# A second product turned around, sparse rows for more tokens, and an earlier choice of experts (hybrid decoder layer, one core)

## What is computed

```python
def block(xb):                       # 128 tokens, 8 heads, top 16 of 128 x 128 experts
    qry = (xb @ w_q).reshape(TB, PEER_HEADS, PEER_D_KEY)
    s1 = jnp.einsum('thd,nd->thn', qry[..., :half], keys_1)
    s2 = jnp.einsum('thd,nd->thn', qry[..., half:], keys_2)
    v1, i1 = lax.top_k(s1, K)
    v2, i2 = lax.top_k(s2, K)
    cand = (v1[..., :, None] + v2[..., None, :]).reshape(TB, PEER_HEADS, K * K)
    sc, ci = lax.top_k(cand, K)
    idx = (take(i1, ci // K) * PEER_N_KEYS + take(i2, ci % K))
    gate = jax.nn.softmax(sc, axis=-1)
    act = jax.nn.gelu(jnp.einsum('thed,td->the', u_table[idx], xb), approximate=False)
    return jnp.einsum('the,thed->td', gate * act, v_table[idx])
```

## Time and profile before

| | |
|---|---|
| three runs | 1499.63, 1503.68, 1505.55 us, median 1503.68 |
| the profiled execution | 1502.88 us, its span 1501.1 us |
| mean granted clock of TensorE | 0.991 of full speed |
| busy share: PE, DVE, POOL, ACT | 98%, 78%, 45%, 43% |
| DMA | 410.28 MB, 273 GB/s on the mean |
| TensorE instructions of the second product | 2304 matmuls of 512 columns |
| TensorE instructions of the first product | 3072 of 352 columns, 768 of 128 |

### The profile page before, as it was taken

How to read it: one execution, slowest core, us unless ns; L and a number is a source line. 1 busy time by engine, 2 the same in 40 slices (tenths; PEclk the granted TensorE clock), 3 DMA queues, 4 the chain that set the end, 5 groups by cost and what they waited for, 6 DMA issues and landing times.

```text
span 1501.1 us, 23329 instructions
## 1 busy us (share of the span) xinstructions
PE 1467.1 (98%) x8045; PEld 1304.6 (87%) x8045; DVE 1174.9 (78%) x2373; ACT 640.7 (43%) x1055; POOL 672.8 (45%) x390
## 2 busy tenths in 40 slices
PE   7999989899999999999999999999999999999998
PEld 6879658788999999999999999988888888888887
DVE  4747473278999999989899899568878878877876
ACT  4463453222333333457777766433233233224221
POOL 2423140133586678865455454134433433443441
PEclk9999979999999999999999999999999999999999
DMA  7400202220569989999999999699999999999993
GB/s 263 148 29 1 113 1 74 85 85 16 191 224 351 328 307 351 412 376 358 370 366 375 373 358 387 238 378 376 386 350 354 346 347 352 347 352 349 350 344 123
DMA packets 183961, 410.28 MB, mean 273 GB/s; under 512 B 12852, under 2 KB 108852, under 8 KB 182360
## 3 DMA queue, kind: packets, MB, share of 16 engines
q1 hardware_dynamic: 142296, 258.46, 48.6%
q0 software_dynamic: 41600, 151.03, 26.5%
HBM read 361.12 MB, written 48.30 MB: 273 GB/s over the span
## 4 chain that ended last, share of the span: by engine, by line
PE 79%; DVE 9%; DMA 7%; POOL 2%; issue 1%; ACT 1%; SPq 0%; DVEq 0%; ACTq 0%; POOLq 0%
PE banks L1987 21%; PE banks L1760 16%; PE banks L2055 12%; PE banks L2056 12%; PE banks L2057 12%; DMA u_rows<-in_u,idx 7%; DVE gate_rows L1621 3%; DVE u_rows L1566 2%; POOL u_lo L739 2%; PE banks L2026 1%; PE banks L1968 1%; DVE u_lo L1549 1%; DVE oh L1617 1%; PE banks L1787 1%; PE banks L1832 1%
## 5 line engine op out<-in xcount | busy, mean ns | idle before, releaser
L787 POOL DMA_INDIRECT v_rows<-in_v,idx x128 | 204.2, 1596 | 325.5 <-DVE x_res L1705 273.9
L2055 PE MATMUL banks<-v_hi,w_hi 128*128 128x512 f32 x768 | 298.9, 389 | 0.0
L2056 PE MATMUL banks<-v_lo,w_hi 128*128 128x512 f32 x768 | 298.8, 389 | 0.0
L2057 PE MATMUL banks<-v_hi,w_lo 128*128 128x512 f32 x768 | 298.8, 389 | 0.0
L1118 ACT ACTIVATE v_hi<-v_raw 128x1024 fp32r<-128x1024 f32 x128 | 126.4, 1050 | 327.0 <-PE banks L2057 294.5
L755 POOL DMA_INDIRECT u_rows<-in_u,idx x160 | 189.2, 1182 | 137.6 <-DVE z L1566 105.2
L1643 DVE TENSOR_TENSOR v_lo<-v_raw,v_hi 128x1024 fp32r<-128x1024 f32 x128 | 153.4, 1219 | 96.3 <-ACT v_hi L1118 96.3
L739 POOL TENSOR_TENSOR u_lo<-u_raw,u_hi 128x1024 fp32r<-128x1024 f32 x66 | 164.6, 2497 | 86.4 <-ACT u_hi L1004 46.0
L1987 PE MATMUL banks<-h_lo,u_hi 128*128 128x352 f32 x1024 | 196.2, 326 | 0.0
L1987 PE MATMUL banks<-h_hi,u_hi 128*128 128x352 f32 x1024 | 189.2, 327 | 0.0
L1987 PE MATMUL banks<-h_hi,u_lo 128*128 128x352 f32 x1024 | 184.2, 322 | 2.8 <-DVE u_lo L1549 2.8
(11 more groups left out here) (277 smaller groups left out, 2086.9 us busy)
## 6 DMA issues: line engine op xcount, KB each, us to landing
u_raw<-in_uT SPq DMA_DIRECT2D x128, 512.0 KB
v_raw<-in_v SPq DMA_DIRECT2D x128, 512.0 KB
gate_scratch<-stage SPq DMA_DIRECT2D x12, 2048.0 KB
gates<-gate_scratch SPq DMA_DIRECT2D x29, 768.0 KB
act_scratch<-act_out SPq DMA_DIRECT2D x116, 176.0 KB
act_in<-act_scratch SPq DMA_DIRECT2D x29, 704.0 KB
wi_raw<-in_w_in SPq DMA_DIRECT2D x8, 1024.0 KB, 7.0
wq_raw<-in_w_q SPq DMA_DIRECT2D x8, 1024.0 KB, 5.7
```

The costliest lines, as they stand in the source:

```text
L787: nc.gpsimd.indirect_dma_start(v_rows[s % V_ROWS][:], None, v_flat, bass.IndirectOffsetOnAxis(ap=idx0[:, s:s + 1], axis=0)).then_inc(vg_in ...
L2055: mm(y, w, v_hi[q][:, j, ds], start=first and j == 0, stop=False)
L2056: mm(y, w, v_lo[q][j][:, ds], start=False, stop=False)
L2057: end = mm(y, w_lo[q][:, j, t * P:(t + 1) * P], v_hi[q][:, j, ds], start=False, stop=last and j == GROUP - 1)
```

## The change

**Second product turned.** v becomes stationary, w moves: per group 8 chunks of the width x 4 blocks x 3 passes = 96 matmuls of 352 columns. The result is y transposed, 8 chunks in 8 banks (`Y_BANKS` has eight; the chunk's columns NE to ND hold the 352 tokens). At the end ACT copies each chunk to `yT`, TensorE turns it by 24 transposes (`turn`) into six banks, and DVE adds these to x; x is stored in six half tiles, not three whole ones.

**Sparse v rows for the 32 tokens.** Their gates no longer go to DRAM: CHUNKS 12 -> 11, BATCHES 96 -> 88 (the last trip of the gate stage has 8 batches, the last four blocks before POST none), the weights have 352 columns. Instead 32 more gathers bring v rows (kind "w"); DVE scales and sums them in `acc_b` (z1 x g1 as the scale; g1 comes by 4 small DMAs on SP's queue before the gate stage), and 8 matmuls with `fold` add the four groups of 32 partitions into the y banks before the last group. Kind "v" is block 0's v rows. One list `ALL_DOTS` now orders all 320 gathers; 10 of "w" stand in POST (1, 1, 1, 1, 2, 2, 1, 1), the other 22 and 128 of "v" in groups 1 to 30, five in each.

**Block 0 chosen early.** Score jobs become `s0` (block 0, emptied by DVE) and two `s13` (block 1; blocks 2 and 3), which ACT copies to SBUF. DVE does block 0's top-k of a head with those of block 1 and of one earlier head of block 2; after head 3 it chooses experts of the first four heads of block 0, and POOL starts gathering. The rest of the top-k's and choosing is spread over the first product's blocks (`routing`). Eight dots lie in the query stage, 72 in blocks 0 to 71 and 80 in the gate stage (before: 0, 71, 81, and 8 in POST). POOL makes u_lo of blocks 0 to 31 alone and gathers between. wq_lo gets three buffers; the last wq_lo stands on POOL's queue behind `idx_ready` and four gathers.

The diff, cut to its core:

```diff
-CHUNKS = ND // CHUNK
+CHUNKS = NA // CHUNK
-BATCHES = ND // BATCH
+BATCHES = NA // BATCH
-POOL_FIRST, SHARE_FROM = 16, 20
+POOL_FIRST, SHARE_FROM = 32, 32
+EARLY = 8
+for _n in [x for x in range(30) if x % 3 < 2]:
+    DOTS[_n] = "a"
-for _n in [*range(PRE - 25, PRE, 2), *range(PRE + 1, PRE + 32, 2), PRE + 4, PRE + 14, PRE + 24]:
+for _n in [*range(PRE - 19, PRE, 2), *range(PRE + 1, PRE + 32, 2), *range(PRE + 4, PRE + 28, 4)]:
     DOTS[_n] += "b"
-for _n in [*range(PRE - 14, PRE, 4), *range(PRE + 32, POST)]:
+for _n in range(PRE + 32, PRE + 44):
     DOTS[_n] += "a"
+POST_ADDS = [1, 1, 1, 1, 2, 2, 1, 1]
+ALL_DOTS += "w" * (NE - ALL_DOTS.count("w")) + "v" * SLOTS
+FREE_PIECE = 2650
 PIECE_SIZE = 1800
-Y_BANKS = (4, 5, 6, 7, 0, 1)
+Y_BANKS = (4, 5, 6, 7, 2, 3, 0, 1)
...
-        jobs += [(("s12", h, i), "D") for i in range(2)]
+        jobs += [(("s0", h), "D")] + [(("s13", h, i), "A") for i in range(2)]
...
@@ gpsimd
+            for h in range(PH - 1):
+                split_query(h)
+            pool.wait_ge(idx_ready, 1)
+            for s in range(U_ROWS // 2):
+                gather_u(s)
+            split_query(PH - 1)
+            for s in range(U_ROWS // 2, U_ROWS):
+                gather_u(s)
             for n in range(POOL_FIRST):
                 split_u(n)
+                if n < EARLY:
+                    gather_u(U_ROWS + n)
+                elif DOTS[n - EARLY]:
+                    gather_u(U_ROWS + dots_before(n - EARLY))
...
@@ scalar, after the heads' scores
+                free(copy(scores_1[:, h, :], bank(j)[:, 0:2 * NK]), j)
+                free(copy(scores_23[:, :, h, :], bank(j).rearrange("p (t e) -> p t e", t=2)), j)
...
+                if h + 2 == PH:
+                    for b in (2, 3):
+                        emptied(act, LAST_ON[b])
+                    nc.scalar.activation(h2_first, h2_nat[:, 0, :], ACT.Copy).then_inc(h2_placed, 1)
...
+            for c in range(KD):
+                act.wait_ge(y_done, c + 1)
+                copy(yT[:, c, :], ps[:, Y_BANKS[c], 0:ND]).then_inc(yT_ready, 1)
...
@@ vector
+            for h in range(PH // 2):
+                top_k(0, h)
+                top_k(1, h)
+                if h:
+                    top_k(2, h - 1)
+            for _ in choose(0, 0, PH // 2):
+                pass
+            top_k(2, PH // 2 - 1)
+            for h in range(PH // 2, PH):
+                top_k(0, h)
+                if h > PH // 2:
+                    top_k(1, h - 1)
+                if h >= PH - 2:
+                    for _ in range(EARLY // 2):
+                        dot()
...
-                nc.vector.tensor_copy(w32[:, :, 0:NE], head).then_inc(w_ready, 1)
...
@@ tensor, second product
-                for o in range(6):
+                for c in range(KD):
+                    if last and c == 6:
+                        turn(0, range(4))
+                    if last and c == 7:
+                        turn(1, (4, 5))
+                    ds = slice(c * P, (c + 1) * P)
+                    y = ps[:, Y_BANKS[c], NE:ND]
                     for j in range(GROUP):
-                        w = w_hi[q][:, j, t * P:(t + 1) * P]
-                        mm(y, w, v_hi[q][:, j, ds], start=first and j == 0, stop=False)
-                        mm(y, w, v_lo[q][j][:, ds], start=False, stop=False)
+                        mm(y, v_hi[q][:, j, ds], w_hi[q][:, j, :], start=first and j == 0, stop=False)
+                        mm(y, v_hi[q][:, j, ds], w_lo[q][:, j, :], start=False, stop=False)
+                        end = mm(y, v_lo[q][j][:, ds], w_hi[q][:, j, :], start=False, stop=last and j == GROUP - 1)
...
+            pe.wait_ge(dot_done, U_DOTS + NE)
+            for c in range(KD):
+                mm(ps[:, Y_BANKS[c], 0:NE], acc_b[:, c * P:(c + 1) * P], fold[:], start=False, stop=False)
             second(GROUPS - 1, 1, last=True)
```

More of the change, by code:

```diff
@@ L176 @@
 ENGINE_OF = dict(JOBS)
+LAST_ON = [JOBS[max(n for n in range(len(JOBS)) if (n + BANK_0) % 8 == b)][0] for b in range(8)]
 NTH = {name: sum(e == eng for _, e in JOBS[: n + 1]) for n, (name, eng) in enumerate(JOBS)}
@@ L595, in main @@
                         save_gates(i - 1, 1)
+            sp.wait_ge(tri_ready, 2 * (TB - 1) + 1)
+            for y in range(P // NE):
+                sp.dma_start(g1[y * NE:(y + 1) * NE, :], tri[0:NE, 0, 0, y * NE:(y + 1) * NE]).then_inc(g1_in, 16)
             main(0)
@@ L1092, in main @@
                     n = i * MAIN_BODY + (PRE + j)
-                    take_gates(i, 2 * j, first)
-                    if not (last and j == MAIN_BODY - 1):
+                    if not last or i * MAIN_BATCHES + 2 * j < BATCHES:
+                        take_gates(i, 2 * j, first)
+                    if not last or i * MAIN_BATCHES + 2 * j + 3 < BATCHES:
                         one_hot(i, 2 * j + 3)
@@ L1491, in choose @@
                 settle()
-                for h in range(PH):
+                for h in range(h0, h1):
                     step(nc.vector.max(sc_v[:, t, h, 0:8], cand[:, h, :]))
@@ L1961, in _ @@
                 emptied(pe, ("qry", h, 1))
-                for i in range(2):
-                    o = start(("s12", h, i))
-                    for tt in range(2):
+                for j, blocks in ((("s0", h), (0,)), (("s13", h, 0), (1,)), (("s13", h, 1), (2, 3))):
+                    o = start(j)
+                    for tt, t in enumerate(blocks):
                         for s in range(2):
                             c0 = (2 * tt + s) * NK
-                            t = 2 * i + tt
                             last = mm(o[:, c0:c0 + NK], qryT[:, (2 * h + s) % 3, t * P:(t + 1) * P],
@@ L2027, in gate_matrices, with main @@
                 last.then_inc(gate_done, 1)
-            def main(i, first=False):
+            def main(i, first=False, last=False):
                 for j in range(MAIN_BODY):
@@ L2032, in main, with turn @@
                                 lambda b=b: gate_matrices(i, b, first and b < 4))
-                               for b in BATCHES_IN[j]]
+                               for b in BATCHES_IN[j] if not last or i * MAIN_BATCHES + b < BATCHES]
                     first_product(i * MAIN_BODY + (PRE + j), j, i, PRE + j, MAIN_BODY, between=between)
             main(0, True)
-            with pe.Fori(1, MAIN_TRIPS) as i:
+            with pe.Fori(1, MAIN_TRIPS - 1) as i:
                 main(i)
+            main(MAIN_TRIPS - 1, last=True)
             for n in range(POST, E_BLOCKS):
                 first_product(n, n, 0, n, 1, ring=2)
+            def turn(half, chunks):
+                for c in chunks:
+                    pe.wait_ge(yT_ready, max(c + 1, 3 * half + 3))
+                    for t in range(3):
+                        o = ps[:, Y_BANKS[3 * half + t], c % 4 * P:(c % 4 + 1) * P]
+                        end = nc.tensor.transpose(o, yT[:, c, t * P:(t + 1) * P], ident)
+                        if c % 4 == 3:
+                            end.then_inc(yT_turned, 1)
             def second(g, q, first=False, last=False):
```

424 lines of the change are left out of this document (236 added, 188 removed).

## The result

The changed kernel takes 1539.4 us (median of 4 runs, 1534.6 to 1547.0), the kernel before 1504.6 (median of 4 runs on the same chip): a ratio of 1.024, 95% interval 1.019 to 1.029. It is 2.4% slower where I had forecast 1% faster, and 15 us above the top of my range. The profiled execution took 1536.9 us, span 1535.1.

The account below looks back on a forecast made before the run. TensorE was taken to bound the kernel, with DMA close behind. From 1502.9 us the terms -7.1, +4.5, -1, -15.8 and +5.5 sum to -13.9, so 1489 us; range 1467 to 1524, the forecast's own 1480 to 1499.

Parts of the forecast that it names:

- (c): First product and sparse dots: POOL's splits thinly covered, 0 for holes there; -1 us in all, bounds -6 and +5.
- (b): Query stage: early half choosing makes TensorE wait for a bank and the first block wait; +4.5 us, bounds 0 and +12.
- (a): Gate stage: 88 batches of gate matrices instead of 96, at 0.89 us each, saving 7.1 us.
- (d): Second product: DMA bounds a group at 387 GB/s, 15.9 us; -15.8 us in all, bounds -35 and +30.
- (e): End of kernel: new fold matmuls, transposes, copy and adds cost +5.5 us, bounds +2 and +9.
- a DMA ceiling of 350 GB/s: Second product: lower end of the rival that DMA sustains less than 387 GB/s, giving 1535 us; rival's chance 0.12.
- a hole at the start that sets the slow pace: First product: POOL falls behind, TensorE stops and matmuls then start every 166.7 ns, giving 1522 us; chance 0.2.
- TensorE as the bound of the second product: Second product: DMA carries 405 GB/s, so groups take 15.2 us; 1470 us, or 1465 without holes; chance 0.13.
- the fourth rival: Matmuls of 352 columns start every 149 ns by the skill's rule, 14.3 us a group; no chance of its own given.

Follow-up runs that it names:

- late_choice: Changed kernel with query stage, order of choosing, dots and first-product schedule as before the change; turned product and sparse v rows stay: 1505.0 us, ratio 0.9997.
- relief: Changed kernel with 20 early dots moved to blocks 104 to 119, routing spread, and half choosing put behind head 4's top-k: 1540.9 us, ratio 1.025.
- short_dots: Changed kernel with dots of u rows over 512 of 1024 elements up to block 71, all gathers left: 1523.9 us, ratio 1.012.
- half_later: Changed kernel with DVE's choosing for block 0's first four heads put behind the top-k of head 4: 1537.8 us, ratio 1.023.
- half_rows: Changed kernel with 2 KB instead of 4 KB fetched by each descriptor of the v row gathers, same instructions: 1519.2 us, ratio 1.009.

## Why the prediction was wrong

**(c), the first product, is the step that failed:** 0 put down, +31.4 measured, bounds -6 and +5. I counted POOL's splits and gathers against 3.8 us a block, called the cover thin, and never added up DVE's work over the stretch. Its terms stood in my own text: three top_k's per head for four leave the rest for later, at 2.9 us each. Ten of them are 29 us, against 10 us that were free. The splits and the half choosing that leave the stretch take most of that back; what the counts leave is some 18 us more, and the longer instructions, some 14 us by my estimate, which no term of mine held, come on top. Instead I wrote that early choosing "costs and gives nothing beyond this". I had looked at the right wait (POOL late for u_lo) and at the wrong engine for it. late_choice and relief show it; short_dots shows that the rate up to block 31 alone, with a small sum, costs 24 us.

**(b), the query stage,** was mis-sized: +9.2 for +4.5, inside its bounds. The bank wait came where I put it, 4.52 us for 2.2, for DVE ended its half choosing near 368.5 and not at 366. What I left out is the clock behind the hole: 3.75 and 2.74 us for eight matmuls instead of 1.98, 2.5 us more. The stretch behind it has a granted clock of 0.62 on the mean, part at 1.2 and part at 2.4 GHz:

```profile
373.30:380.00 6.70, 6.68 (x19) 5.33 (x20) 6.28 (x37) 0.00 (x0) 6.22 (x4) 0.62 0.59 218
```

And half_later showed the next wait at once, POOL's gathers ahead of the last wq_lo, of which I had said that it would be just in time.

**(a), the gates:** -7.1 put down; the stage gave -1.6. The count was right, 704 gate matmuls for 768. The slow pace took the rest: 0.18 us in each of the 39 blocks with batches that the kernel before did at the fast pace, and 1 us in the six blocks ahead of them, 8 us together. Shorter waits in this stage (4.2 us for 6.4) gave 2 us back. That a term could be lost to the pace stood only in a rival, and tied to a hole.

**(d), the second product.** The ceiling was right: 387 forecast, 388 GB/s at share 1.05 from 1150 to 1475 us. By that 1981 matmuls in 325 us are 15.75 us a group for 15.9. Yet the second product with its end gave -5.1 for -10.3. The start is where it went: I let the first groups run at TensorE's pace, and they have the holes: from 1013.6 to 1163 us 867 matmuls start, which at 158.3 ns are 137.2 us and took 149.4; 7.2 of that are waits for v_lo. Half_rows, whose waits for v_lo come to 1.6 us for 13.8 in the whole product, puts those down to transfers too. The figure of the Trainium skill ("DMA: Bandwidth & Descriptors", Specifications), about 358 GB/s, is again passed by a sustained 388.

**(e):** from the last product matmul to the end 5.7 us for 4.4; my 2.8 more and "some 7 us" were a little high.

**The rivals.** The nearest times, 1535 (a DMA ceiling of 350 GB/s) and 1522 (a hole at the start that sets the slow pace), would both have been luck. The lower ceiling didn't come about: 388. The hole came, 17.8 us against 2.67 at 884, but it didn't set the pace: slow from 472 us on, fast from 486, slow from 490, fast behind 501 and behind the 17.8 us hole, and slow again from the transposes of the tables at 681, where TensorE doesn't stop. I priced the pace and not the hole itself. TensorE as the bound of the second product holds only with fewer bytes (half_rows, 15.2 us a group), and no long stretch starts its matmuls of 352 columns closer than 158.3 ns, so the fourth rival's faster start isn't seen either.

## What to carry to other kernels

When a change moves work in time, add up every engine's work for each stretch, before and after, and hold it against the stretch's length; a mean of 78% busy hides a stretch at 96%, and 28 us more in it cost 31. Leave room in that sum: here nearly half of the growth, by my estimate, was no new instruction, but old ones that took longer. Do the same by the point at which another engine needs a release, since a schedule counted in blocks can be too dense in its first half while its sum fits. And an idle engine is no free place for work whose operands come late over a nearly full DMA: here 20 dots moved there cost 33 to 37 us in the profiles.

## What the chip showed

While POOL was at its splits, some of DVE's instructions took several times as long: seven that write `cand` took 6.07 us at 444 (POOL: two splits from 444.6 on), and one `picked` 8.23 at 473 (two splits from 473.0 on), where a later one of the same shape took 3.49:

```profile
444.17 6.07 DVE L1557 TENSOR_TENSOR cand<-best_v 128x128 f32<-128x128 f32 x7
...
472.91 8.23 DVE L1586 TENSOR_TENSOR picked<-pay,sc_f 128x3200 f32<-128x3200 f32 x1
...
533.73 3.49 DVE L1586 TENSOR_TENSOR picked<-pay,sc_f 128x3200 f32<-128x3200 f32 x1
```

The 8.23 us are the 3.49 and 4.74 more, and POOL's two splits took 4.73 together, as if DVE had waited them out. That is one case; that POOL's work is the cause, and which of its operations, wasn't tried. Matmuls of 352 columns have two paces at granted clock 1.00, 158.7 and 166.3 ns, over hundreds of microseconds each. The pace turned in either direction at stops, and without a stop at the first batches of late_choice and at the transposes of the changed kernel. The cause isn't known.
